# Sample rows of a projection in two column halves of TensorE, and feature groups of 363, 363 and 362 columns

## The chip, the cores and the metric

One core of a Trainium2 chip runs the whole program. The metric is the device time of one execution in microseconds (us). All numbers are float32.

## The reference

One inference step of a one-layer decoder for a prompt (1024 tokens) and samples (8 sequences of 8 tokens, 64 rows): 1088 token rows of width 1024.

```python
h = _rmsnorm(x, norm1_g) * (1.0 + sc1) + sh1
q, k, v, qi, ki, wi, hq, hf, hi, hg = _project(h, w_in, idx_k_g, pos)   # z = h @ w_in, split into columns
a = _rmsnorm(attend(q, k, v, qi, wi, ki), attn_out_g)                   # indexer picks 256 keys per query
r, s_T = _hgrn2(hq, hf, hi, hg, lb, hg_out_g, s0)                       # gated linear recurrence
mix = jnp.einsum('bte,ed->btd', jnp.concatenate([a, r], axis=-1), w_out)
x = x + gt1 * mix
x = x + gt2 * _moe(_rmsnorm(x, norm2_g) * (1.0 + sc2) + sh2, ...)       # 16 experts, 2 per token
```

The change touches the product `h @ w_in` alone: 1088 rows times 3656 columns, with a contraction of 1024, so eight matmuls of 128 each add up to one result.

## The kernel before, in words

The program is a row of stages with a barrier of all engines between them: modulation, front (the projection, with the indexer's scores and its selection beside it), prompt attention, sample attention, recurrence, output projection, router, experts, final norm. The change is in `front` and in `projection_groups`, which lists its work.

The normalised input stands transposed in on-chip memory as `hT`, 128 partitions by 8 blocks (`a`) by 1088 tokens, the 64 sample tokens last. Six blocks of 512 weight columns are worked off in turn, after a first one:

- The first block (the indexer's queries) is done by `first(i)`, for each of nine tiles of tokens (`ROWS`: eight of 128 rows and one of 64, `NS`). Line 1060 is its matmul of 512 columns, line 1063 a small one of 72 columns into the next bank; ScalarE copies both out (lines 1206 and 1208).
- `project(n)` (line 1075) does one group out of `groups`, eight matmuls. There are 60 groups in six blocks. In "token" blocks (`QC`, `KC`, `HI0`, `HG0`, kinds `z` and `tok`) a group is one tile of tokens: tokens are the weights that are loaded into the array, and 512 columns of the weight matrix stream past them, so nine groups, the last of which has 64 rows and uses 64 of the array's 128 columns. In "feature" blocks (`HF0`, `HQ0`) it is the other way around: 128 features are the loaded weights and tokens stream, since the recurrence wants features on partitions. A feature block has four column blocks `f`, each with three groups of 512, 512 and 64 tokens.

`evict(n)` on ScalarE copies group `n` out of its bank: into `z` for the first two blocks (lines 1217 to 1220), else with a function into one of four `stage` buffers (line 1229), from where SyncE stores it (line 1017). Two banks are used in turn, so group `n` waits for the copy of the group two before it (`pev`).

The order on TensorE is written out: after group `n` come the pieces that its slot has. In slots 2 to 9 these are six pieces each of the prompt's index scores (`score`, line 1124; ScalarE applies relu at line 1265, VectorE weighs and adds at lines 1444 and 1447); in slots 11 to 27 one unit each of the samples' scores (lines 1133, 1143, 1153); at the third and sixth group of each block a part of a modulation product (line 1086) and one slot on its sum (line 1089). VectorE searches thresholds meanwhile (lines 1359 to 1390).

SyncE has one queue for the loads of weights (`load`, line 962; `load_ada`, line 967), which fill two buffers `wp` in turn, each when the products that read it are done, and for the stores. At the end of the stage SyncE waits for the last copy, issues its store and those of the keys, and all engines meet at the barrier.

Of the kernel before, what the change touches and what calls it, by code (L numbers as in the profile page):

```python
# [15 lines left out]
ACT = mybir.ActivationFunctionType  # L16
AX = mybir.AxisListType

P = 128
D = 1024  # L20
KD = D // P
SEQ = 1024
DB, DS = 8, 8
NS = DB * DS
# [135 lines left out]
QC, KC, VC, QIC, KIC, WIC = 0, 512, 768, 1024, 1536, 1600  # L160
# [230 lines left out]
def paired(ap, order):  # L391

    return ap.rearrange(order, a=2, g=2, x=2)
# [441 lines left out]
def ada_after(groups, last, n):  # L835

    j = groups[n][0]
    l = n - (last[j - 1] + 1 if j else 0)
    return [(kind, 2 * j + x) for x, at in enumerate((PART1, PART2)) for kind, d in (("part", 0), ("total", 1)) if l == at + d]


def projection_groups(k, wp):


    t, hT, z = k.t, k.ar.view(HT, KD, T), k.ar.view(O_Z, NT, NA)
    w_v = t["w_in"].rearrange("o (a p) n -> p (o a) n", p=P)
    chunks = ((QC, "z", None), (KC, "z", None), (HF0, "feat", t["hf"]), (HQ0, "feat", t["hq"]), (HI0, "tok", t["hv"]), (HG0, "tok", t["hg"]))
    groups = []
    for j, (c0, kind, dst) in enumerate(chunks):
        b = (j + 1) % 2  # L850
        if kind == "feat":
            for f in range(GH):
                for c, n in ((0, 512), (512, 512), (1024, NS)):
                    groups.append((j, P, n, (lambda a, f=f, b=b: wp[b][:, a, f * P:(f + 1) * P]),
                                   (lambda a, c=c, n=n: hT[:, a, c:c + n]), dst[:, f, c:c + n]))
        else:
            for i in range(NT):
                groups.append((j, ROWS[i], 512, (lambda a, i=i: hT[:, a, i * P:i * P + ROWS[i]]),
                               (lambda a, b=b: wp[b][:, a, :]), None if dst is None else dst[0:ROWS[i], i, :]))
    sources = [w_v[:, :, c[0]:c[0] + 512] for c in chunks]  # L860
    return sources, groups


def front(k):


    nc, t, ar, ps = k.nc, k.t, k.ar, k.ps
    hT, z = ar.view(HT, KD, T), ar.view(O_Z, NT, NA)
# [3 lines left out]
    wp = [ar.view(O_W + b * KD * 512, KD, 512) for b in range(2)]  # L872
# [5 lines left out]
    def new(*d, **kw):  # L878
        nonlocal o
        v = ar.view(o, *d, **kw)  # L880
        o += int(np.prod(d))
        return v
# [19 lines left out]
    stage = [new(512) for _ in range(4)]  # L902
# [6 lines left out]
    kk = ar.view(O_H, NT, HD)  # L909

    sources, groups = projection_groups(k, wp)
    ada = modulation_chunks(t)[ADA1:]
    last = {gr[0]: n for n, gr in enumerate(groups)}
    ring, after = [], [ada_after(groups, last, n) for n in range(len(groups))]
# [22 lines left out]
    s = {n: k.sem("fr_" + n) for n in names}  # L937
# [20 lines left out]
    with nc.Block() as block:  # L958
# [92 lines left out]
        def _(pe):  # L1051
            def first(i):
                r, b = ROWS[i], 2 * (i % 3)
                pe.wait_ge(k.s_mod, done[i])
                if i == 0:
                    pe.wait_ge(k.s_ahead, 32)
                if i >= 3:
                    pe.wait_ge(s["z1"], 2 * (i - 2))
                for a in range(KD):
                    ins = pe.matmul(ps[0:r, b, :], hT[:, a, i * P:i * P + r], wp[0][:, a, :], start=(a == 0), stop=(a == KD - 1))  # L1060
                ins.then_inc(s["m1"], 1)
                for a in range(KD):
                    ins = pe.matmul(ps[0:r, b + 1, 0:WK], hT[:, a, i * P:i * P + r], wk[:, a, :], start=(a == 0), stop=(a == KD - 1))
                ins.then_inc(s["m1"], 1)

            def project(n):
                j, m, cols, lhs, rhs, dst = groups[n]
                if n == 0:
                    pe.wait_ge(s["z1"], 2 * NT)
                if n == 0 or groups[n - 1][0] != j:  # L1070
                    pe.wait_ge(s_w[(j + 1) % 2], 16 * loads["w", j])
                if ring[n] >= 2:
                    pe.wait_ge(s["pev"], ring[n] - 1)
                for a in range(KD):
                    ins = pe.matmul(ps[0:m, ring[n] % 2, 0:cols], lhs(a), rhs(a), start=(a == 0), stop=(a == KD - 1))  # L1075
                ins.then_inc(s["pmm"], 1)

            def modulate(kind, a):
# [108 lines left out]
            for i in range(NT):  # L1187
                first(i)
            for n in range(len(groups)):
                project(n)  # L1190
                for m in slot_pieces(n, NPC):
                    score(m)
                u = slot_unit(n, UNITS)
                if u is not None:
                    sample(u)
                    if u == UNITS:
                        fresh()
                for job in after[n]:
                    modulate(*job)

        @block.scalar
        def _(act):
            def first(i):
                r, b = ROWS[i], 2 * (i % 3)
                act.wait_ge(s["m1"], 2 * i + 1)
                act.activation(z[0:r, i, QIC:QIC + 512], ps[0:r, b, :], ACT.Copy).then_inc(s["z1"], 1)
                act.wait_ge(s["m1"], 2 * i + 2)
                act.activation(z[0:r, i, KIC:KIC + WK], ps[0:r, b + 1, 0:WK], ACT.Copy).then_inc(s["z1"], 1)  # L1208

            def evict(n):  # L1210
                j, m, cols, lhs, rhs, dst = groups[n]
                act.wait_ge(s["pmm"], ring[n] + 1)
                bank = ring[n] % 2
                if dst is None:
                    i, c = n % NT, (QC, KC)[n // NT]
                    if c == QC and i < NT - 1:
                        act.activation(paired(z[:, i, c:c + 512], "p (a g x d) -> p a g x d")[:, 0], paired(ps[:, bank, :], "p (a x g d) -> p a g x d")[:, 0], ACT.Copy)
                        act.activation(paired(z[:, i, c:c + 512], "p (a g x d) -> p a g x d")[:, 1], paired(ps[:, bank, :], "p (a x g d) -> p a g x d")[:, 1], ACT.Copy).then_inc(s["pev"], 1)
                    else:
                        act.activation(z[0:m, i, c:c + 512], ps[0:m, bank, :], ACT.Copy).then_inc(s["pev"], 1)  # L1220
                    return
                before = len([q for q in stored if q < n and q % 4 == n % 4])
                if before:
                    act.wait_ge(s_st[n % 4], 16 * before)
                if n == NZ:
                    act.wait_ge(s["ks"], 2)
                    act.wait_ge(s["sq"], 1)
                func, scale = {2: (ACT.Sigmoid, 1.0), 3: (ACT.Copy, float(DK) ** -0.5), 4: (ACT.Copy, 1.0), 5: (ACT.Silu, 1.0)}[j]
                act.activation(stage[n % 4][0:m, 0:cols], ps[0:m, bank, 0:cols], func, scale=scale).then_inc(s["pev"], 1)  # L1229

            def modulated(kind, a):
                at = turn_of[kind, a]
# [71 lines left out]
            for i in range(NT):  # L1304
                first(i)
            for m in range(2):
                act.wait_ge(s["ms"], m + 1)
                n, a, b = parts[m]
                act.activation(ksd[0:n, a:b], kss[0:n, a:b], ACT.Sqrt).then_inc(s["ksd"], 1)
            for n in range(len(groups)):  # L1310
                evict(n)
                for m in slot_pieces(n, NPC):
                    score(m)
                u = slot_unit(n, UNITS)
                if u is not None:
                    sample(u)
                    if u == UNITS:
                        fresh()
                for job in after[n]:
                    modulated(*job)  # L1320
# [1427 lines left out]
```

## Time and profile before

| | |
|---|---|
| median of 3 runs | 1901.65 us (1897.7 to 1906.0) |
| the profiled execution | 1895.58 us, its span 1893.7 us |
| mean granted TensorE clock | 0.920 |
| TensorE busy | 1623.2 us, 86% |
| VectorE busy | 840.8 us, 44% |
| ScalarE busy | 384.3 us, 20% |
| GpSimd busy | 207.0 us, 11% |

The span goes from the first to the last instruction of one execution. An engine's busy time is the union of its instructions' times. TensorE's matmuls (PE) overlap one another, so the distance from one start to the next tells what one costs; weight loads (PEld) run beside them. "Granted clock" is the share of TensorE's full clock that it was given.

### The profile page before, as it was taken

The page shows a single profiled execution, that of the slowest core. Times are in us where ns is not written, and L with a number is a line of the kernel's source. Part 1 is how long each engine was busy: PE and PEld are TensorE (multiplying, and loading weights), DVE is VectorE, ACT ScalarE, POOL GpSimd, SP SyncE. Part 2 cuts the span into 40 slices and gives each one's busy share as a digit, 9 for nine tenths or more (in the row PEclk, how much of TensorE's full clock was granted, in tenths as well). Part 3 has the DMA queues.
Part 4 walks back from the last instruction along what each step waited for, and adds up shares of the span by engine and source line. Part 5 has one row for each costly group of instructions (what it writes and reads, how often), then busy time and mean ns, then how long its engine had stood idle before and what let it go on. Part 6 is the DMA issues. An engine that isn't in the chain of part 4 may idle for free. (4 is left out here: it accounts for less than half of the span.)

```text
span 1893.7 us, 20779 instructions
## 1 busy us (share of the span) xinstructions
PE 1623.2 (86%) x7594; PEld 792.0 (42%) x7595; DVE 840.8 (44%) x1926; ACT 384.3 (20%) x762; POOL 207.0 (11%) x181
## 2 busy tenths in 40 slices
PE   4999999999999889989952959992599999999970
PEld 3544333444433367765422725542233333333320
DVE  3133579999998044543217624337111111111116
ACT  4003432321111145422234321210000000000002
POOL 0001001100000000000002620000011111111112
PEclk9998999999999979989985879995799999999995
DMA  9112113423333220043625063211989999999934
GB/s 330 46 51 74 45 45 124 152 76 119 115 128 126 92 92 1 1 182 138 263 73 193 2 215 108 101 60 57 390 261 353 378 354 348 349 346 325 327 79 188
DMA packets 128280, 317.53 MB, mean 168 GB/s; under 512 B 15393, under 2 KB 22841, under 8 KB 125626
## 3 DMA queue, kind: packets, MB, share of 16 engines
q1 hardware_dynamic: 112010, 233.30, 34.7%
q0 software_dynamic: 16176, 82.98, 13.2%
q8 instruction: 60, 0.98, 0.2%
q14 instruction: 34, 0.28, 0.0%
HBM read 277.74 MB, written 38.51 MB: 167 GB/s over the span
## 5 line engine op out<-in xcount | busy, mean ns | idle before, releaser
L2505 PE MATMUL banks<-arena 128*64 x1008 | 439.4, 596 | 5.3 <-issue 2.6
L2506 PE MATMUL banks<-arena 128*64 128x512 f32 x1008 | 439.5, 596 | 0.0
L1075 PE MATMUL banks<-arena 128*128 128x512 f32 (+2 forms) x960 | 384.3, 557 | 0.3 <-ACT arena L1208 0.3
L1075 PEld LDWEIGHTS banks<-arena 128*128 128x128 f32 (+1 forms) x960 | 167.5, 188 | 220.2 <-issue 214.6
L2505 PEld LDWEIGHTS banks<-arena 128*64 128x64 f32 x1008 | 136.8, 137 | 283.0 <-issue 283.0
L1359 DVE TENSOR_SCALAR_CACHE_REDUCE arena<-arena 128x384 uint8<-128x384 f32 (+3 forms) x224 | 246.0, 1142 | 3.4
L2506 PEld LDWEIGHTS banks<-arena 128*64 128x64 f32 x1008 | 136.8, 137 | 0.0
L2574 DVE TENSOR_TENSOR arena<-arena,banks 128x256 f32<-128x256 f32 x42 | 15.8, 417 | 263.6 <-PE banks L2506 263.6
L2085 PE MATMUL banks<-arena 128*128 128x512 f32 (+1 forms) x288 | 127.7, 602 | 2.9 <-DMA arena<-in_w_out 2.9
L2556 ACT ACTIVATE arena<-banks 128x512 f32<-128x512 f32 x21 | 12.5, 597 | 466.7 <-PE banks L2506 466.7
L1626 DVE CUSTOM_DVE_ANT_0 arena<-banks,arena 128x512 f32<-128x512 f32 (+3 forms) x96 | 51.4, 575 | 81.1 <-PE banks L1562 81.1
L2585 DVE SCALAR_TENSOR_TENSOR arena<-banks,arena 128x1024 f32<-128x1024 f32 x21 | 27.0, 1284 | 129.5 <-PE banks L2506 129.5
L2085 PEld LDWEIGHTS banks<-arena 128*128 128x128 f32 (+1 forms) x288 | 53.2, 188 | 71.0 <-issue 70.6
L1585 PEld LDWEIGHTS banks<-arena 128*128 128x128 f32 x576 | 71.1, 199 | 26.7 <-ACT arena L1680 13.8
L1585 PE MATMUL banks<-arena 128*128 128x64 f32 x576 | 77.4, 286 | 0.0
L1060 PE MATMUL banks<-arena 128*128 128x512 f32 (+1 forms) x144 | 66.4, 616 | 4.5 <-PEq L146 4.5
L1229 ACT ACTIVATE arena<-banks 128x512 f32<-128x512 f32 (+2 forms) x42 | 22.1, 527 | 228.2 <-PE banks L1075 228.2
L1447 DVE SCALAR_TENSOR_TENSOR arena<-arena 128x512 f32<-128x512 f32 (+3 forms) x84 | 53.8, 641 | 30.5 <-ACT arena L1265 25.5
L2459 POOL DMA_INDIRECT arena<-tmp_x,arena x22 | 21.0, 955 | 400.8 <-DVE arena L2585 400.5
L1673 ACT ACTIVATE arena<-arena 128x128 f32<-128x128 f32 (+7 forms) x64 | 49.1, 768 | 48.0 <-DVE arena L1626 48.0
L1048 POOL TENSOR_TENSOR arena<-arena 9x512 f32<-9x512 f32 x12 | 15.9, 1321 | 328.5 <-ACT arena L1239 328.5
L1124 PE MATMUL banks<-arena 64*128 64x512 f32 (+3 forms) x192 | 41.9, 547 | 9.2 <-ACT arena L1265 9.1
(409 smaller groups left out, 1928.2 us busy)
## 6 DMA issues: line engine op xcount, KB each, us to landing
arena<-in_w SPq DMA_DIRECT2D x63, 2048.0 KB, 12.9
arena<-in_ada_w SPq DMA_DIRECT2D x12, 2048.0 KB, 8.5
arena<-in_w_in SPq DMA_DIRECT2D x7, 2048.0 KB, 7.7
arena<-in_ada_final_w SPq DMA_DIRECT2D x4, 2048.0 KB, 8.1
arena<-in_x_prompt SPq DMA_DIRECT2D x4, 1024.0 KB, 8.3
arena<-in_w_out SPq DMA_DIRECT2D x2, 2048.0 KB, 10.3
arena<-in_x_prompt SPq DMA_DIRECT2D x8, 512.0 KB, 4.2
tmp_yslot<-arena POOLq DMA_DIRECT2D x8, 512.0 KB, 5.2
```

Of the source, the lines that this page charges most:

```text
L1060: ins = pe.matmul(ps[0:r, b, :], hT[:, a, i * P:i * P + r], wp[0][:, a, :], start=(a == 0), stop=(a == KD - 1))
L1075: ins = pe.matmul(ps[0:m, ring[n] % 2, 0:cols], lhs(a), rhs(a), start=(a == 0), stop=(a == KD - 1))
L1124: ins = pe.matmul(ps[:, 2 + 2 * (m % 2) + v, 0:w], qiT[i % 2][hs, p, :], kiT[hs, c * 512:c * 512 + w], start=True, stop=True)
L1359: ch.mark(ve.tensor_scalar(junk[u], accs_[u], bound(u), None, ALU.is_ge, ALU.add, accum_out=cnt[0:rows, u:u + 1]))
L1447: ve.scalar_tensor_tensor(dst, rl[m % 2][:, v, 0:w], wt, dst, ALU.mult, ALU.add).then_inc(s["acc"], 1)
L1585: ins = pe.matmul(ps[:, 6 + i % 2, h * HD:(h + 1) * HD], PT[q % 4][:, v, :], z[:, u, VC + (h // 2) * HD:VC + (h // 2 + 1) * HD], start=(u ...
L1626: ve.tensor_tensor_reduce(L[n % 3][:, x, c * 512:c * 512 + w], ps[:, 2 * (m % 2) + x, 0:w], ar.view(ACC_AT[n // 4] + c * 512, w), 1.0, low ...
L1673: act.activation(L[n % 3][:, x, 0:N], L[n % 3][:, x, 0:N], ACT.Exp, bias=low[:, 0, col], scale=-1.0, accum_out=den[:, col]).then_inc(s["e" ...
L2085: ins = pe.matmul(ps[0:r, OUT[n % 3], :], mT[i % 2][:, a, 0:r], wo[:, a, c * 512:(c + 1) * 512], start=(a == 0), stop=(a == KD - 1))
L2505: pe.matmul(ps[0:HP, bank, :], x[:, 0:HP], Wt[:, bass.ds(at, 1), off:off + width].rearrange("p o a -> p (o a)"), **kw)
L2506: return pe.matmul(ps[HP:P, bank, :], x[:, HP:P], Wt[:, u, off:off + width], **kw)
L2585: ve.scalar_tensor_tensor(Y[b], ps[:, 5:7, :].rearrange("p a b -> p (a b)"), wslot[:, bass.ds(n, 1)] if not isinstance(n, int) else wslot[ ...
```

## The change

Where a group has 64 rows (`r == NS` in `first`, `m == NS` in `project`), each of its eight matmuls becomes two of 256 streamed columns. The same 64 tokens are loaded into the array's left and right half of columns; the first 256 weight columns stream past the one, the last 256 past the other, and the results lie in partitions 0 to 63 and 64 to 127 of the same bank. There are five such groups. ScalarE copies each of them out in two instructions, which put the two halves side by side again.

The feature blocks' token ranges become 0 to 362, 363 to 725 and 726 to 1087.

```diff
-                for c, n in ((0, 512), (512, 512), (1024, NS)):
+                for c, n in ((0, 363), (363, 363), (726, 362)):
...
                 for a in range(KD):
-                    ins = pe.matmul(ps[0:r, b, :], hT[:, a, i * P:i * P + r], wp[0][:, a, :], start=(a == 0), stop=(a == KD - 1))
+                    if r == NS:
+                        for v in range(2):
+                            ins = pe.matmul(ps[v * NS:(v + 1) * NS, b, 0:256], hT[:, a, i * P:i * P + r], wp[0][:, a, v * 256:(v + 1) * 256], start=(a == 0), stop=(a == KD - 1))
+                    else:
+                        ins = pe.matmul(ps[0:r, b, :], hT[:, a, i * P:i * P + r], wp[0][:, a, :], start=(a == 0), stop=(a == KD - 1))
...
                 for a in range(KD):
-                    ins = pe.matmul(ps[0:m, ring[n] % 2, 0:cols], lhs(a), rhs(a), start=(a == 0), stop=(a == KD - 1))
+                    if m == NS:
+                        for x in range(2):
+                            ins = pe.matmul(ps[x * NS:(x + 1) * NS, ring[n] % 2, 0:256], lhs(a), rhs(a)[:, x * 256:(x + 1) * 256], start=(a == 0), stop=(a == KD - 1))
+                    else:
+                        ins = pe.matmul(ps[0:m, ring[n] % 2, 0:cols], lhs(a), rhs(a), start=(a == 0), stop=(a == KD - 1))
...
-                act.activation(z[0:r, i, QIC:QIC + 512], ps[0:r, b, :], ACT.Copy).then_inc(s["z1"], 1)
+                if r == NS:
+                    act.activation(z[0:r, i, QIC:QIC + 256], ps[0:NS, b, 0:256], ACT.Copy)
+                    act.activation(z[0:r, i, QIC + 256:QIC + 512], ps[NS:P, b, 0:256], ACT.Copy).then_inc(s["z1"], 1)
+                else:
+                    act.activation(z[0:r, i, QIC:QIC + 512], ps[0:r, b, :], ACT.Copy).then_inc(s["z1"], 1)
...
-                act.activation(stage[n % 4][0:m, 0:cols], ps[0:m, bank, 0:cols], func, scale=scale).then_inc(s["pev"], 1)
+                if m == NS:
+                    act.activation(stage[n % 4][0:m, 0:256], ps[0:NS, bank, 0:256], func, scale=scale)
+                    act.activation(stage[n % 4][0:m, 256:512], ps[NS:P, bank, 0:256], func, scale=scale).then_inc(s["pev"], 1)
+                else:
+                    act.activation(stage[n % 4][0:m, 0:cols], ps[0:m, bank, 0:cols], func, scale=scale).then_inc(s["pev"], 1)
```

The copies into `z` in `evict` are split in the same way.

## Rows read from the trace of the kernel before

**Rows 1.** The page: busy time by engine; granted clock, in tenths, in 40 slices

```profile
PE 1623.2 (86%) x7594; PEld 792.0 (42%) x7595; DVE 840.8 (44%) x1926; ACT 384.3 (20%) x762; POOL 207.0 (11%) x181
...
PEclk9998999999999979989985879995799999999995
```

**Rows 2.** Busy time by stretch: the sum over eight stretches from 47 to 651 us

```profile
sum 604.00, PE 587.62 PEld 257.76 DVE 416.11 ACT 134.59 POOL 31.23; mean PE 73.45 PEld 32.22 DVE 52.01 ACT 16.82 POOL 3.90
```

**Rows 3.** The timeline (start, duration, what, idle before) at the front's end

```profile
644.28 0.14 PEld L1075 LDWEIGHTS banks<-arena 128*64 128x64 f32 x1 [0.29 <-issue]
...
649.43 0.14 PEld L1075 LDWEIGHTS banks<-arena 128*64 128x64 f32 x1 [0.29 <-issue]
650.49 0.59 ACT L1229 ACTIVATE arena<-banks 64x512 f32<-64x512 f32 x1 [6.41 <-PE banks L1075]
651.11 0.45 SPq L1017 DMA_DIRECT2D tmp_hg<-arena  x1
...
656.62 3.41 DVE L1647 COPY arena<-banks 128x256 f32<-128x256 f32 x8 [46.44 <-PE banks L1594]
```

**Rows 4.** The timeline of TensorE in slots with sample scores

```profile
337.05 7.08 PE L1075 MATMUL banks<-arena 128*64 128x512 f32 x16
344.07 0.66 PE L1133 MATMUL banks<-arena 128*128 128x128 f32 x4
...
355.87 7.13 PE L1075 MATMUL banks<-arena 128*128 128x512 f32 x16
362.84 0.60 PE L1133 MATMUL banks<-arena 128*128 128x128 f32 x4
...
365.23 2.00 PE L1075 MATMUL banks<-arena 128*128 128x64 f32 x16
367.06 0.61 PE L1133 MATMUL banks<-arena 128*128 128x128 f32 x4
```

**Rows 5.** Groups of instructions by line and shape: busy time, mean ns, idle before

```profile
L1075 PE MATMUL banks<-arena 128*64 128x512 f32 x64 | 28.3, 595 | 0.0
```

**Rows 6.** The timeline of TensorE in the sample attention

```profile
888.22 2.12 PE L1798 MATMUL banks<-arena 128*64 128x512 f32 x4
890.15 1.92 PE L1826 MATMUL banks<-arena 128*64 128x256 f32 x16
892.00 0.66 PE L1810 MATMUL banks<-arena 128*128 128x128 f32 x4
```

**Rows 7.** Groups of instructions by line and shape, ScalarE, in the front

```profile
L1229 ACT ACTIVATE arena<-banks 128x512 f32<-128x512 f32 x32 | 19.1, 597 | 206.6 <-PE banks L1075 206.6
L1217 ACT ACTIVATE arena<-banks 128x256 f32<-128x256 f32 x8 | 3.1, 384 | 47.9 <-PE banks L1075 47.9
L1229 ACT ACTIVATE arena<-banks 128x64 f32<-128x64 f32 x8 | 1.8, 227 | 8.7 <-PE banks L1075 8.7
```

**Rows 8.** The timeline around the first block's sample tile

```profile
119.56 7.08 PE L1060 MATMUL banks<-arena 128*64 128x512 f32 x16
126.47 1.16 PE L1063 MATMUL banks<-arena 128*64 128x72 f32 x16
127.67 0.22 ACT L1208 ACTIVATE arena<-banks 64x72 f32<-64x72 f32 x1 [0.41 <-PE banks L1063]
...
128.01 0.22 DVE L1411 TENSOR_TENSOR arena<-arena 64x64 f32<-64x64 f32 x1 [5.53 <-ACT arena L1208]
```

**Rows 9.** The timeline of VectorE around the second block's sample tile

```profile
237.52 5.68 DVE L1447 SCALAR_TENSOR_TENSOR arena<-arena 128x512 f32<-128x512 f32 x7
...
247.76 0.42 DVE L1444 TENSOR_SCALAR arena<-arena 128x384 f32<-128x384 f32 x1 [4.56 <-ACT arena L1265]
```

**Rows 10.** The timeline around one weight load, and line 967's times to landing

```profile
445.76 0.43 SPq L967 DMA_DIRECT2D arena<-in_ada_w  x1
...
460.56 1.92 PE L1086 MATMUL banks<-arena 128*32 128x512 f32 x16
...
DMA to landing us min/median/max: 7.7/8.0/9.0
```

More of the change, by code:

```diff
@@ L1218, in evict @@
                         act.activation(paired(z[:, i, c:c + 512], "p (a g x d) -> p a g x d")[:, 1], paired(ps[:, bank, :], "p (a x g d) -> p a g x d")[:, 1], ACT.Copy).then_inc(s["pev"], 1)
+                    elif m == NS:
+                        act.activation(z[0:m, i, c:c + 256], ps[0:NS, bank, 0:256], ACT.Copy)
+                        act.activation(z[0:m, i, c + 256:c + 512], ps[NS:P, bank, 0:256], ACT.Copy).then_inc(s["pev"], 1)
                     else:
```

## The prediction

> **What bounds the kernel now.** I read the page's totals first, then busy time by stretch, then the order of events at the end of the stage that the change touches, and then the groups of instructions inside it. TensorE is busy for 86% of the span [rows 1], and in the projection stage (47 to 651 us) for 587.62 of 604 us [rows 2]. The granted clock by slices is 9 tenths or more through nearly all of it, so mostly the 2.4 GHz level. Whatever TensorE no longer does there comes out of the stage, unless something else ends later. Nothing else does at present: VectorE's first instruction of the next stage stands at 656.62 with 46.44 us of idle time before it, so VectorE was done at 610.2 us [rows 3]. TensorE's last weight load starts at 649.43, and one record of 0.43 us later ScalarE copies the result out (650.49), SyncE issues the last stores (from 651.11) and the next stage begins. That tail of some 6 us hangs on TensorE's end and stays. So the stage's end is TensorE's end, and behind it VectorE leaves 40 us of cover.
>
> **A fact about the records.** A float32 matmul of the program is two records. In a run of 512-column records the weight loads start 0.43 us apart (12 steps from 644.28 to 649.43, 5.15 / 12 = 0.429) [rows 3]. Eight matmuls, one group, take 362.84 - 355.87 = 6.97 us with 128 of the array's columns and 344.07 - 337.05 = 7.02 us with 64 [rows 4]: half the array costs as much as all of it. Start to start is what counts; the durations printed in the rows overlap.
>
> **Part 1, sample rows.** Five groups have the 128*64 form: four of line 1075 (64 records) [rows 5] and one of line 1060 (16 records) [rows 8]. Each now issues 32 records of 256 columns, alternately in the two column halves. The trace has this very form: line 1826 runs 16 records of 128*64 with 256 columns, two halves in turn, and takes 892.00 - 890.15 = 1.85 us to the next instruction [rows 6]. If the halves followed each other it would be 16 x 0.215 = 3.4 us, so they run side by side. The 1.85 us are 8 steps of 0.2155 (half of 0.429 and a little) and 0.13 us for entering and leaving the form. For 16 steps I take 16 x 0.2155 + 0.13 = 3.58 us. Saved per group: 7.02 - 3.58 = 3.44 us; five groups: 17.2 us. The best case is half of 7.02 us (3.51), 0.4 us more over the five. The bad end is no overlap, 7.0 us, nothing saved.
>
> A rule of the Trainium skill speaks against this part: its page "TensorEngine Tiling (Array Packing)", section Key Properties, says that a change of tiling mode drains the engine. By rows a half-width group costs 0.05 us more than a full one, and line 1826's 16 records 0.13 us beyond their columns, once per group. If a drain came with each step (rival d), the sum would be another.
>
> ScalarE's copy of such a group becomes two of 256 columns: 0.384 us stands for 128x256 and 0.597 for 128x512 [rows 7], so 0.77 in place of 0.60. Under a matmul group of 3.58 us, with two banks in turn, that is hidden. It shows once, in the last group of the stage, where store and barrier wait for the copy: +0.17 us. In the first group the copy must be done before the next big group; the small group of line 1063 lies between (126.47, its own copy starts at 127.67), 1.2 us, so it is covered [rows 8].
> The same page, section PSUM Bottleneck, warns that the copies out of PSUM don't get faster with tiling; by that the copies could take over from TensorE, but with 0.77 us against 3.58 the rows leave the sum as it is.
>
> Two of the five sit where others could take the gain. After the first (119.56 us) comes a chain of VectorE and SyncE work (norms, rotation, a round trip through memory) for which TensorE waits later. That chain starts at the copies of this very group: VectorE idles 5.53 us until the copy at 127.67 [rows 8], so it moves forward by the whole 3.44. The second stands between two batches of index scores, while VectorE works off its backlog until 237.52 + 5.68 = 243.20; then it idles 4.56 us until the next batch [rows 9]. A group shorter by 3.44 us leaves 1.1 us of that idle time, so the gain holds; if it did not, it would cost up to 3.4 us, which I keep for the range.
>
> **Part 2, feature groups.** Eight feature blocks (two weight blocks with four column blocks each) have groups of 512, 512 and 64 columns and get 363, 363 and 362: the same 24 groups, 1088 columns and 16 records a group. Before: 6.97 + 6.97 + (367.06 - 365.23 = 1.83) = 15.77 us [rows 4]. The 64-column group is the dear one: 1.83 / 16 = 0.114 us per record, where its columns at the 512-column rate would take 0.054; something per record (its weight load of 128 columns) sets it. A record of 363 columns lies between two measured sizes on a straight line, 0.2155 at 256 and 0.429 at 512: 0.2155 + 107 x 0.000834 = 0.305 us, well over 0.114. A group: 16 x 0.305 + 0.1 (what 6.97 holds beyond 16 x 0.429) = 4.98 us; three, one of them a column shorter: 14.93. Saved: 0.84 us, eight times 6.7 us. Where groups follow without score work between them the 0.1 falls away, and it is up to 7.2; I take 6.9.
>
> The trace has no moving operand of 363 columns and none that starts at the 363rd element of a row. The nearest row on where elements lie is line 1798, whose moving operand takes every 16th element: (890.15 - 888.22) / 2 = 0.965 us for a pair of 512 columns, 1.9 ns per column against 0.84 [rows 6]. So the bad end is 363 x 1.9 = 0.69 us per record, +0.385 us x 384 records = +148 us. But the elements are contiguous as in the 512-column groups, and only the first one's place is new; I take the straight line. One extra fetch of that strided kind per record would be 384 x 0.0019 = 0.7 us.
>
> Copies: 0.597 + 0.597 + 0.227 = 1.42 us before [rows 7]; 363 columns on the line between 256 and 512 take 0.47 us, three again 1.42. Store rows of 2048 and 256 bytes become 1452; a buffer is wanted again four groups (20 us) later. Weights: the tightest load is issued at 445.76, lands within 9.0 us, at 454.8, and is wanted at 460.56 [rows 10]; three shorter groups take 0.9 us of the 5.8 us of slack. SyncE's queue keeps its order.
>
> **Sum.** 17.2 + 6.9 - 0.17 = 23.9 us. TensorE's end moves from 650 to 626 us; VectorE's, 610 now, moves forward too, since its search begins after the scores. Later stages are not touched and start earlier by as much. The profiled execution took 1895.58 us (span 1893.7): 1871.7. The median of the runs shown, 1901.65, lies 6.1 us above it; less 23.9 it is 1877.7, rounded to 1877.5.
>
> **Rivals.**
> (a) The halves don't run side by side in this code, the change not doing what it says: only part 2 counts, -6.7 us, 1894.9. For it: both halves here load the same block of hT as weights, where line 1826 had different ones. Against it: rows 6, with the same form, bank and order. 4%.
> (b) A moving operand that starts off the old boundaries streams slower. Part 2 turns from -6.9 into 384 records x the excess. From 0.062 us per record (20%) all of the 23.9 us is eaten; at half the strided excess (0.19 us) the kernel is at 1877.5 + 74 = 1951. For it: line 1798 shows that the place of elements can set TensorE's rate. Against it: there each element lies apart, here only the first one's place differs. 5%, of which 1% stays within no change.
> (c) The freed time turns into a wait: scores, weights, or stretches at the 1.2 GHz level that fall differently (the clock's slices after the stage hold 7s and 5s [rows 1]). A gain cut by half gives 1889.5; 6%, of which a third passes into no change.
> (d) Each of the 16 steps pays the 0.13 us: 16 x 0.3455 = 5.5 us a group, 7.5 us saved in place of 17.2: 1887.2. Against it: line 1826, where 8 steps paid it once. 2%. [...]
> My forecast has 83%, with a range of its own of 1870 to 1885, the scatter of the runs (1897.7 to 1906.0) included. For 8 in 10 I reach over (d) and up to (c): 1868 to 1889. A change of under 0.5% (9.5 us) can't be told from none. Faster: 0.83 + 0.04 + 0.02 = 0.89; same: 0.04 + 0.01 + 0.02 = 0.07; slower: 0.04.
>
> **What would show it.** Right: pairs of 256-column records at lines 1060 and 1075 that step by 0.215; sample groups of 3.6 us; feature groups of 4.9 to 5.0 us, three alike; VectorE's first instruction of the next stage at 633 in place of 656.62. Wrong: records of 363 columns stepping by more than 0.31, pairs stepping by 0.43, weight loads that wait for DMA in the feature blocks, or VectorE ending the stage.

## The result, and the profile after

The changed kernel took 1873.66 us (median of 4 runs, 1872.1 to 1875.4) beside 1899.68 us before (4 runs): a ratio of 0.987, interval 0.9845 to 0.9895, so 20 to 29 us less. Two more sets gave 0.9861 (0.9827 to 0.9895) and 0.9854 (0.9828 to 0.9879). The forecast was 1877.5 us, with 23.9 us saved.

The profiled execution took 1872.1 us, its span 1870.2, so 23.5 us less than the profiled one before. First the stages: busy time by stretch, of the kernel before and then of the one after. The lines are the front stage, the prompt attention and all that follows; each gives its length, the engines' busy time with instruction counts, TensorE's granted clock, and DMA.

```profile
47.52:655.06 607.54, 587.62 (x1929) 257.75 (x1930) 415.96 (x953) 134.67 (x232) 31.23 (x28) 0.97 0.26 89
655.06:830.20 175.14, 166.15 (x1104) 124.24 (x1104) 81.77 (x266) 80.48 (x185) 2.85 (x3) 0.91 0.10 39
830.20:1893.70 1063.50, 847.10 (x4384) 394.20 (x4384) 328.59 (x668) 146.82 (x314) 172.74 (x146) 0.89 0.65 227
```

```profile
47.70:629.98 582.28, 562.14 (x2009) 266.59 (x2010) 415.28 (x953) 136.10 (x237) 30.69 (x28) 0.98 0.28 93
629.98:803.03 173.05, 163.08 (x1104) 121.83 (x1104) 81.48 (x266) 80.35 (x185) 2.84 (x3) 0.93 0.10 39
803.03:1870.20 1067.17, 848.93 (x4384) 394.56 (x4384) 329.00 (x668) 146.44 (x314) 172.74 (x146) 0.88 0.65 226
```

The front lost 25.3 us, TensorE's busy time in it 25.5. The stages behind it, which have the same instructions, came out 2.1 us shorter and 3.7 us longer, with the granted clock 0.02 higher and 0.01 lower. Two more traces of the changed kernel have fronts of 583.3 and 579.7 us, so against the one trace of the kernel before the front lost 24.2 to 27.8 us.

The timeline of TensorE in the slots with sample scores, after (start, duration, what), answers to [rows 4]:

```profile
330.31 3.67 PE L1081 MATMUL banks<-arena 128*64 128x256 f32 x32
333.91 0.66 PE L1141 MATMUL banks<-arena 128*128 128x128 f32 x4
...
336.36 5.15 PE L1083 MATMUL banks<-arena 128*128 128x363 f32 x16
341.34 0.60 PE L1141 MATMUL banks<-arena 128*128 128x128 f32 x4
...
343.73 5.16 PE L1083 MATMUL banks<-arena 128*128 128x363 f32 x16
348.72 0.60 PE L1141 MATMUL banks<-arena 128*128 128x128 f32 x4
...
351.11 5.13 PE L1083 MATMUL banks<-arena 128*128 128x362 f32 x16
356.08 0.60 PE L1141 MATMUL banks<-arena 128*128 128x128 f32 x4
```

A sample group takes 333.91 - 330.31 = 3.60 us from its start to the next one's, in place of 7.02. A feature block's three groups take 4.98, 4.99 and 4.97 = 14.94 us in place of 15.77.

The timeline around the first sample tile, after, for [rows 8], and at the end of the front, for [rows 3]:

```profile
117.84 1.90 PE L1067 MATMUL banks<-arena 128*128 128x72 f32 x16
119.67 3.67 PE L1062 MATMUL banks<-arena 128*64 128x256 f32 x32
123.18 1.16 PE L1067 MATMUL banks<-arena 128*64 128x72 f32 x16
...
621.51 3.67 PE L1081 MATMUL banks<-arena 128*64 128x256 f32 x32
...
625.23 0.38 ACT L1245 ACTIVATE arena<-banks 64x256 f32<-64x256 f32 x1 [3.02 <-PE banks L1081]
625.62 0.38 ACT L1246 ACTIVATE arena<-banks 64x256 f32<-64x256 f32 x1
626.03 0.45 SPq L1017 DMA_DIRECT2D tmp_hg<-arena  x1
...
631.53 3.13 DVE L1666 COPY arena<-banks 128x256 f32<-128x256 f32 x8 [28.80 <-PE banks L1613]
```

The first sample group went from 6.91 to 3.51 us. At the end the last copy is in two parts, 625.23 to 626.00; VectorE was done at 631.53 - 28.80 = 602.7, still 22 us before TensorE (621.51 + 3.67 = 625.18), so TensorE's end is the stage's end as before.

### The profile page after: what moved, and what is told of

Its sections match the earlier page's. It is cut to its first block and busy times, and to the rows that moved or that the text cites. A ratio compares the mean times of both kernels' runs of the same rounds, so it can differ in the third digit from the quotient of the medians.

```text
span 1870.2 us, 20944 instructions
## 1 busy us (share of the span) xinstructions
PE 1596.4 (85%) x7674; PEld 798.6 (43%) x7675; DVE 840.2 (45%) x1926; ACT 385.2 (21%) x767; POOL 206.5 (11%) x181
## 3 DMA queue, kind: packets, MB, share of 16 engines
q0 software_dynamic: 16176, 82.98, 13.3%
## 5 line engine op out<-in xcount | busy, mean ns | idle before, releaser
L1083 PE MATMUL banks<-arena 128*128 128x512 f32 (+2 forms) x896 | 348.4, 545 | 0.3 <-ACT arena L1220 0.3
L1083 PEld LDWEIGHTS banks<-arena 128*128 128x128 f32 x896 | 168.0, 191 | 183.7 <-issue 137.5
L2104 PE MATMUL banks<-arena 128*128 128x512 f32 (+1 forms) x288 | 127.3, 600 | 3.0 <-DMA arena<-in_w_out 3.0
L2104 PEld LDWEIGHTS banks<-arena 128*128 128x128 f32 (+1 forms) x288 | 53.1, 187 | 70.8 <-issue 70.2
L1604 PEld LDWEIGHTS banks<-arena 128*128 128x128 f32 x576 | 69.5, 195 | 26.1 <-ACT arena L1699 14.3
L1248 ACT ACTIVATE arena<-banks 128x363 f32<-128x363 f32 (+2 forms) x40 | 20.9, 523 | 207.1 <-PE banks L1083 207.1
L1064 PE MATMUL banks<-arena 128*128 128x512 f32 x128 | 59.3, 618 | 4.0 <-PEq L146 4.0
```

Of the source, the lines that this page charges most:

```text
L1604: ins = pe.matmul(ps[:, 6 + i % 2, h * HD:(h + 1) * HD], PT[q % 4][:, v, :], z[:, u, VC + (h // 2) * HD:VC + (h // 2 + 1) * HD], start=(u ...
L2104: ins = pe.matmul(ps[0:r, OUT[n % 3], :], mT[i % 2][:, a, 0:r], wo[:, a, c * 512:(c + 1) * 512], start=(a == 0), stop=(a == KD - 1))
```

## The experiments

Each timed run stands beside runs of the kernel before on the same chip; its number is its median, how far that lies under the median of those runs, and the ratio with its interval. Executions of one kernel scatter by up to 20 us and more (the kernel before: 1889.6 to 1912.2 in 17), so a difference of a few us is read from a row, not from a median.

### The parts alone

The changed kernel once more (`e0_changed`), and each part without the other:

```diff
 e1_halves_alone: the changed kernel, but
-                for c, n in ((0, 363), (363, 363), (726, 362)):
+                for c, n in ((0, 512), (512, 512), (1024, NS)):
 e2_thirds_alone: the kernel before, but
-                for c, n in ((0, 512), (512, 512), (1024, NS)):
+                for c, n in ((0, 363), (363, 363), (726, 362)):
```

> The changed kernel as it is, beside the parts of it. Theory A (the stage's end is TensorE's end, and every microsecond that TensorE saves there comes out of the time): 24 us below the kernel before. Theory B (the two parts share one piece of slack, or a part of the gain is given back behind the stage): the parts alone add up to more than this run.

> Part 1 alone: sample rows in column halves, feature groups of 512, 512 and 64 columns as before. Theory A: five groups of 3.6 us in place of 7.0, 17 us below the kernel before, and 7 us above the changed kernel. Theory B: the gain is 20 us or more here, since the other part no longer takes from the same slack. Theory C (only the last sample group of the stage counts, the other four disappear in waits for scores and copies): 3.4 us.

> Part 2 alone: feature groups of 363, 363 and 362 columns, sample rows in one piece as before. Theory A: eight times 0.84 to 0.9 us, 7 us below the kernel before. Theory B: more than 7 us, up to what is missing between part 1 and the whole. Theory C (the feature blocks are held by weight loads from memory or by ScalarE's copies): under 2 us.

Measured: the whole 1874.96 us, 26.1 under the kernel before (0.9861, 0.9827 to 0.9895); the halves 1880.75, 20.4 under (0.9899, 0.9864 to 0.9934); the thirds 1887.28, 13.8 under (0.994, 0.9916 to 0.9964). Theory A's 24, 17 and 7 us lie in the intervals (6.8 to 16 us for the last, so at its edge). The two parts add up to 34 by their medians, as theory B had it, but the intervals are wider than the difference. The rows decide. The front with the halves alone, by stretch:

```profile
47.50:635.40 587.90, 567.06 (x2009) 257.01 (x2010) 417.22 (x953) 135.40 (x237) 33.12 (x28) 0.98 0.27 92
```

TensorE's timeline with the halves alone, a sample group and a block's last group:

```profile
327.43 3.67 PE L1081 MATMUL banks<-arena 128*64 128x256 f32 x32
331.04 0.66 PE L1141 MATMUL banks<-arena 128*128 128x128 f32 x4
...
352.20 2.00 PE L1083 MATMUL banks<-arena 128*128 128x64 f32 x16
354.04 0.60 PE L1141 MATMUL banks<-arena 128*128 128x128 f32 x4
```

and with the thirds alone:

```profile
346.06 5.15 PE L1075 MATMUL banks<-arena 128*128 128x363 f32 x16
351.05 0.60 PE L1133 MATMUL banks<-arena 128*128 128x128 f32 x4
```

Each part's groups cost the same alone and together (3.61 and 3.60 us; 4.99 and 4.98), so in the stage neither takes from the other. The front lost 19.6 us with the halves alone (607.5 - 587.9) and 8.8 with the thirds alone (598.7 us in that trace), so all five sample groups and the feature groups count, and theory C falls too.

The granted clock accounts for most of what the medians have beyond that; this is an estimate from the runs' own times and clocks. The 17 executions of the kernel before run from 1912.2 us at a mean clock of 0.912 to 1889.6 at 0.927; a straight line through them gives about 1.2 us less for each 0.001 more. Their mean clock was 0.9180, that of the halves alone 0.9202, of the thirds alone 0.9222, of the whole 0.9205. Set to one clock, the mean gains of 18.5, 12.1 and 26.7 us become 15.9, 7.1 and 23.7: the parts add up to 23.0, so little is left for theory B.

### Sizes of the feature groups

```diff
 e3_384_384_320
-                for c, n in ((0, 363), (363, 363), (726, 362)):
+                for c, n in ((0, 384), (384, 384), (768, 320)):
 e4_512_440_136
-                for c, n in ((0, 363), (363, 363), (726, 362)):
+                for c, n in ((0, 512), (512, 440), (952, 136)):
```

> The changed kernel with feature groups of 384, 384 and 320 columns, which start at the 384th and 768th element. Theory A (a record costs 0.00083 us per column and a little, wherever it starts, as long as that is more than its weight load): the same time as with 363, 363 and 362, within 0.3 us; records of 0.322, 0.322 and 0.269 us. Rival (odd sizes and odd starts cost something per record): faster than the changed kernel, by 3.8 us for each 0.01 us per record.

> The changed kernel with uneven feature groups of 512, 440 and 136 columns. Theory A (the old 64-column group was dear because a record can't be shorter than its weight load of 0.111 us; 136 columns stream for 0.115 us): records of 0.429, 0.369 and 0.115 us, a column block of 14.6 us, the same time as with three equal groups. Rival (equal groups are what helps, since each group covers the slot and the copy behind it alike): 3 to 7 us above the changed kernel.

Measured: 1876.15 us, 25.0 under the kernel before (0.9875, 0.9838 to 0.9912), and 1877.31, 23.4 under (0.9909, 0.9873 to 0.9945). TensorE's timeline with 384, 384 and 320:

```profile
335.32 5.43 PE L1083 MATMUL banks<-arena 128*128 128x384 f32 x16
340.59 0.60 PE L1141 MATMUL banks<-arena 128*128 128x128 f32 x4
...
350.63 4.57 PE L1083 MATMUL banks<-arena 128*128 128x320 f32 x16
355.04 0.60 PE L1141 MATMUL banks<-arena 128*128 128x128 f32 x4
```

and with 512, 440 and 136:

```profile
344.64 6.17 PE L1083 MATMUL banks<-arena 128*128 128x440 f32 x16
350.65 0.60 PE L1141 MATMUL banks<-arena 128*128 128x128 f32 x4
...
353.04 2.12 PE L1083 MATMUL banks<-arena 128*128 128x136 f32 x16
355.00 0.60 PE L1141 MATMUL banks<-arena 128*128 128x128 f32 x4
```

5.27 + 5.26 + 4.41 = 14.94 us for the one, 6.97 + 6.01 + 1.96 = 14.94 for the other, to the hundredth what 363, 363 and 362 take. So odd sizes and odd starts cost nothing, and equal groups are no merit: what counts is that no record streams for less time than its weight load takes. 136 columns take 1.96 us, 64 took 1.83: more than twice the work for 0.13 us. So rival (b) of the prediction is refuted, and part 2's reason, the weight load, has held at one more size.

### The order of the two halves

The same instructions in other orders. In the changed kernel left and right alternate by matmul; here all eight left come first, then the eight right; then blocks of two, and of four.

```diff
 e5_halves_in_turn (the same in first(i))
-                for a in range(KD):
-                    if m == NS:
-                        for x in range(2):
+                if m == NS:
+                    for x in range(2):
+                        for a in range(KD):
 e9_blocks_of_2 (e10_blocks_of_4 with 4 for 2)
+                    for x, a in ((x, a) for c in range(0, KD, 2) for x in range(2) for a in range(c, c + 2)):
```

> The changed kernel, but in the five sample groups all eight matmuls of the left column half come before all eight of the right half: the same instructions in another order. Theory A (two halves run side by side only where their records stand next to each other, since TensorE starts its records in order): groups of 6.9 to 7.0 us, 17 us above the changed kernel, 7 us below the kernel before. Rival (TensorE's halves are two independent engines that take their records out of a queue as they come): groups of 3.6 to 5 us, under 8 us above the changed kernel.

Measured: 1890.92 us, 9.8 under the kernel before (0.9964, 0.9934 to 0.9993). TensorE's timeline, a group later in the stage and the first one:

```profile
334.95 6.32 PE L1082 MATMUL banks<-arena 128*64 128x256 f32 x32
341.20 0.65 PE L1143 MATMUL banks<-arena 128*128 128x128 f32 x4
```

```profile
119.46 5.67 PE L1062 MATMUL banks<-arena 128*64 128x256 f32 x29
124.75 0.40 PE L1068 MATMUL banks<-arena 128*64 128x72 f32 x3
124.96 0.38 PE L1062 MATMUL banks<-arena 128*64 128x256 f32 x1
124.99 0.35 PE L1068 MATMUL banks<-arena 128*64 128x72 f32 x3
125.17 0.38 PE L1062 MATMUL banks<-arena 128*64 128x256 f32 x1
125.18 0.41 PE L1068 MATMUL banks<-arena 128*64 128x72 f32 x4
125.39 0.38 PE L1062 MATMUL banks<-arena 128*64 128x256 f32 x1
```

Neither expectation met it: 6.25 us, short of the 6.9 of strict order and over the 5 of free halves. The front has it five times over: it took 596.6 us in this trace, at least 13.3 more than in the changed kernel's three, where 5 x (6.25 - 3.60) = 13.3. The second fence shows why. The next group (line 1068, which uses the left half) starts at 124.75, while line 1062 still has three records to start on the right. The right half had begun in the same way: in the single records of this trace its first one starts 2.65 us after the group's start in all five groups, beside the left's thirteenth, with three of the left still to start. That makes 12 + 16 = 28 steps for the 32 records, 28 x 0.2155 = 6.03 us, and 0.2 us for entering and leaving the form. The Trainium skill's page "TensorE: Matmul & The Clock Gate", Part 3, section "The mechanism", says of matmuls "strict FIFO, no reordering"; in these rows a record of line 1068 starts before three of line 1062 that stand ahead of it in the program, so here the measurement decides against it. From this came theory D: TensorE looks past three waiting records, and no further.

> The changed kernel, with the sample groups' matmuls in blocks of two: two of the left half, two of the right, and so on (four records each). Theory D, formed from the run with the halves one after the other (there the right half's first record started when the left half had three records to go, so TensorE looks past three waiting records and no further): the right half's first record can start beside the left half's first, so groups of 3.6 us as in the changed kernel. Theory A in its strict form (records start in the order of the program): steps in which only one half works, 4.5 us or more.

> The same with blocks of four matmuls (eight records). Theory D: the right half starts four steps after the left and loses about as much again at the second block, some 20 steps of 0.2155 us and 0.13, so groups of 4.3 to 4.5 us, between the changed kernel's 3.6 and the 6.2 of the halves one after the other. Theory A in its strict form: 5.5 us or more. A look-ahead that grows with the block: 3.6 us.

One execution each, 1877.24 and 1880.58 us. The groups, blocks of two and then of four:

```profile
329.85 3.73 PE L1080 MATMUL banks<-arena 128*64 128x256 f32 x32
333.51 0.66 PE L1141 MATMUL banks<-arena 128*128 128x128 f32 x4
```

```profile
332.10 4.70 PE L1080 MATMUL banks<-arena 128*64 128x256 f32 x32
336.73 0.66 PE L1141 MATMUL banks<-arena 128*128 128x128 f32 x4
```

3.66 us with blocks of two, as theory D says, and 4.63 with blocks of four, 0.1 to 0.3 over it and far from both others. In the single records of the latter, in all five groups, each new block starts 0.92 us after the one before it, beside that one's fifth record, with three still to start. Four steps of 0.2155 are 0.86, so each change of half costs 0.06 us more, and that is what theory D's sum left out: 3 x 0.92 + 8 x 0.2155 = 4.48, and 0.15 for entering and leaving the form. So the look-ahead is three records in every change of half that these runs have, and alternating by one or two matmuls is what makes the halves free. Each record has its own weight load, so these runs don't tell which of the two is counted.

### Further in the same direction

Two edits that these results suggest. The first cuts the first block's 584 weight columns into 456 and 128 in place of 512 and 72, so that the small matmul streams about as long as its weights load (the sample tile's two halves then have 228 columns; loads and copies follow). The second does the sums of the modulation, each one matmul of 512 columns that uses 9 of the array's columns, in four column quarters of the array.

```diff
 e6_456_128
-                        ins = pe.matmul(ps[0:r, b, :], hT[:, a, i * P:i * P + r], wp[0][:, a, :], ...)
+                        ins = pe.matmul(ps[0:r, b, 0:456], hT[:, a, i * P:i * P + r], wp[0][:, a, 0:456], ...)
...
-                    ins = pe.matmul(ps[0:r, b + 1, 0:WK], hT[:, a, i * P:i * P + r], wk[:, a, :], ...)
+                    ins = pe.matmul(ps[0:r, b + 1, 0:128], hT[:, a, i * P:i * P + r], wk[:, a, :], ...)
 e7_sum_quarters
-                    ins = pe.matmul(ps[0:NC, at % 2, :], sel[:, 0:NC], cP, start=True, stop=True)
+                    for v in range(4):
+                        ins = pe.matmul(ps[32 * v:32 * v + NC, at % 2, 0:P], sel[:, 0:NC], cP[:, v * P:(v + 1) * P], start=True, stop=True, tile_position=(0, 32 * v))
```

> The changed kernel with the first block's 584 weight columns cut into 456 and 128 in place of 512 and 72 (of the 72, each record costs its weight load of 0.111 us where its columns would take 0.062). Theory A: records of 0.382 and 0.111 us, 16 x 0.047 = 0.75 us less for each of eight full tiles, the sample tile 0.4 us more (its second group loads 64 columns of weights and was not held by them), in all 5.6 us below the changed kernel. Rival (the 72-column group is held by something else than its weight load, say by the copies): no change, or slower since it streams more.

> The changed kernel with the twelve sums of the modulation (one matmul of 512 columns that uses 9 of the array's columns, 0.95 us) cut into four matmuls of 128 columns in four column quarters, and four copies in place of one. Theory A: 0.95 us become 0.4, twelve times 0.55, so 6 us below the changed kernel, less some tenths of a us where ScalarE's longer copies (4 x 0.28 us for 0.58) are waited for. Rival (in the slots with scores ScalarE is the bound): 2 us or less.

Measured: 1869.65 us, 31.0 under the kernel before (0.9861, 0.9823 to 0.9898), and 1871.29, 29.4 under (0.9861, 0.9827 to 0.9894); the changed kernel had the ratio 0.9861 too, so neither gain can be told from the time. TensorE's timeline with 456 and 128:

```profile
67.08 6.29 PE L1064 MATMUL banks<-arena 128*128 128x456 f32 x16
73.20 1.95 PE L1067 MATMUL banks<-arena 128*128 128x128 f32 x16
74.98 5.52 PE L1064 MATMUL banks<-arena 128*128 128x456 f32 x14
```

and with the sum in quarters:

```profile
317.95 0.41 PE L1098 MATMUL banks<-arena 128*9 128x128 f32 x8
318.29 7.13 PE L1083 MATMUL banks<-arena 128*128 128x512 f32 x16
```

128 columns take 1.78 us (74.98 - 73.20) where 72 took 1.74 in the changed kernel's trace (110.93 - 109.19, also before a group of the full form), so the streamed columns hardly set it. With half the weights (the 128*64 form of line 1067 in the rows around the first sample tile) 72 columns take 1.16 us with their tail in place of 1.90, so the weight load does. A sum takes 0.34 us (318.29 - 317.95) in place of 0.95. On TensorE both are there; the fronts took 579.2 and 576.3 us, where the changed kernel's three traces have 579.7 to 583.3. Both together, with the changed kernel on the same chip:

> The changed kernel with the first block cut into 456 and 128 columns and with the sums of the modulation in quarters. Theory A (every microsecond of TensorE in this stage counts, and what the two edits saved alone adds up): by their traces 4.7 us in the first block and 5.2 us in the sums, so 9 to 10 us below the changed kernel; VectorE still ends before TensorE, with about 19 us to spare. Rival (the copies on ScalarE, longer in both, are waited for): 6 us or less.

> The changed kernel once more, beside the version with both further edits on the same chip. Theory A: 24 us below the kernel before, and 9 to 10 us above that version; the front stage takes 582 to 584 us.

Measured: 1870.56 us for both edits, 26.1 under the kernel before (0.986, 0.9833 to 0.9886), and 1869.98 for the changed kernel, 26.7 under (0.9854, 0.9828 to 0.9879). So the expected 9 to 10 us are not in the time. The profiled executions (1870.36 and 1869.85 us) show where the gain went in that pair: front and prompt attention, of the version with both edits, then of the changed kernel.

```profile
48.45:620.45 572.00, 547.68 (x2082) 265.94 (x2082) 413.86 (x953) 140.89 (x273) 31.50 (x28) 0.98 0.28 95
620.45:799.73 179.28, 169.99 (x1105) 126.55 (x1105) 81.41 (x266) 80.80 (x185) 2.84 (x3) 0.89 0.10 38
```

```profile
48.05:627.77 579.72, 558.81 (x2010) 265.43 (x2010) 415.32 (x953) 135.99 (x237) 30.68 (x28) 0.99 0.28 93
627.77:800.79 173.02, 163.09 (x1105) 121.78 (x1105) 81.47 (x266) 80.32 (x185) 2.84 (x3) 0.93 0.10 39
```

The front is 7.7 us shorter (VectorE was done at 595.1 us, 20 us before TensorE), and the prompt attention, with the same instructions, 6.3 us longer at a granted clock of 0.89 in place of 0.93. The rival named ScalarE's copies, so neither expectation held: the gain was made in the front and given back at the lower clock of the next stage. It was not this one execution alone: the six of the version with both edits were granted 0.916 to 0.920 over their spans, the five of the changed kernel 0.920 to 0.923. The means differ by 0.0049, and the kernel before gives 1.2 to 1.6 us for each 0.001 on the three chips used, so the clock cost the version some 6 to 8 us, by this estimate. The halves alone have a long attention in their profile too:

```profile
635.40:816.70 181.30, 173.24 (x1105) 129.72 (x1105) 81.75 (x266) 80.80 (x185) 2.84 (x3) 0.86 0.10 38
```

That execution (1889.15 us) is one of two at 1888 and 1889, while the other four lie at 1878.6 to 1881.0. The time at which the front ends does not decide it: fronts that ended at 630.0, 630.2 and 630.6 us (the changed kernel, 512-440-136 and 384-384-320) were followed by attentions of 173.0, 181.2 and 171.0 us, and the changed kernel's three traces, with fronts that end from 627.8 to 631.0, have 173.0 each. What does decide it, these runs don't settle. A version that beats the changed kernel for sure was not found.

## Why the prediction was right, point by point

- What bounds: right. The front shortened by what TensorE saved, VectorE ended at 602.7 us, 22 us ahead, and the tail behind TensorE's end stayed. One reading was loose: from the last weight load to the copy lay 1.06 us (650.49 - 649.43), not one record of 0.43; no term hangs on it.
- Part 1: 3.44 us a group were forecast; 7.02 - 3.60 = 3.42 in the slots with sample scores, and 6.91 - 3.51 = 3.40 in the first group. That makes 17.1 us against 17.2. The form's own cost of 0.13 us came once per group, so rival (d), a drain at every step, fell, and rival (a) with the 3.60. The rule that the prediction names against this part is of a change of mode; both halves are of one form, 128*64, so a step from one to the other is none, and the rule gives no drain at every step.
- The copies: 0.77 us against the forecast 0.77, hidden but for the last.
- The two places where the gain might have been lost: neither lost it. After the second sample tile no wait was added; with the halves alone the front is 19.6 us shorter, which takes all five groups.
- Part 2: 4.98 us a group were forecast, 4.98, 4.99 and 4.97 came; 0.83 us a block where score work lies between, so 6.6 us over eight (the forecast took 6.9, with a little more where no score work lies between). The straight line between 256 and 512 columns holds at 320, 363, 384 and 440. Rival (b), at 5%, came to nothing.
- The sum: 23.9 us forecast. The groups give 17.1 + 6.6 - 0.17 = 23.5. The profiled pair has 25.3 in the front and 23.5 in the whole, the medians 26.0, 26.1 and 26.7. That the pair comes so close in the whole is in part luck: the front has more than the groups give, beside a clock of 0.98 in place of 0.97, and the stages behind it gave 1.6 us back. Rival (c), the clock, was priced as a loss of half the gain; here it acted both ways, and between traces it moved the prompt attention alone by 10.6 us.

## What to carry to other kernels

In these traces a float32 matmul's record costs its streamed columns (0.00083 us each) or its weight load, whichever is longer. For 128 columns of weights that load is 1.78 / 16 = 0.111 us, as long as 0.111 / 0.00083 = 134 streamed columns. So cut a row of columns so that no piece falls below that, in equal pieces or not. A group that fills half of the array's columns cost as much as a full one (7.02 us beside 6.97); two halves side by side took 3.60, if their matmuls alternate in the program by one or two. And where a few us are at stake, read the gain from the stage's own rows, since the clock of a later stage can hide a gain or feign one; or compare times beside the granted clock of each execution.

## What the runs showed of the hardware that was not expected

- TensorE starts a record of the array's free half past three waiting ones of the other half, across groups and out of the program's order: 32 records in 28 steps, 6.25 us, with all of one half ahead of the other; blocks of two matmuls 3.66 us, of four 4.63, alternating 3.60.
- Odd widths and starts of the moving operand cost nothing: 14.94 us for 363, 363 and 362, for 384, 384 and 320, and for 512, 440 and 136.
- The prompt attention takes 171.0 to 181.6 us with the same instructions over all these traces, as its granted clock goes from 0.96 to 0.86.
- The time of one and the same kernel follows its mean granted clock: 1912.2 us at 0.912, 1889.6 at 0.927. Set to one clock (an estimate), the parts of the change add up to the whole.
